# A hybrid GLA and RWKV-7 trunk: the first chunk spread over the opening, the block products put right behind the scores, the output tiles' last step moved back, the combined weights loaded from ScalarE's queue

## The reference, cut to what matters

```
h = rms_norm(x, norm_pre);  p = h @ w_in
# GLA group -> o_gla (4 heads, recurrence per token), gated by silu
prev = shift(p_shift);  xm = p_shift + mu * (prev - p_shift)          # token shift
r, kr, vr, wd, ad = split(xm)
w = exp(-0.606531 * sigmoid(w0 + tanh(wd) @ w_up));  a = sigmoid(a0 + ad @ a_up)
kk = normalised(kr * k_k);  kr = kr * (1 + (a - 1) * k_a)
S = S * (w - kk^T (a kk)) + v^T k;   y = S r                          # RWKV-7, 8 heads of 64
y = groupnorm(y) + sum(r * kr * r_k) * v;   o_rwkv = y * silu(z_r)
m = concat(o_gla, o_rwkv) @ w_out;   x = x + rms_norm(m, norm_post)
```

## Time and profile before

| | us |
|---|---|
| median of 3 runs | 2319.01 |
| lowest and highest | 2316.41, 2319.48 |
| the profiled execution | 2315.25 |
| its span | 2313.5 |
| TensorE busy | 2242.2 (97%) |
| VectorE busy | 1448.1 |
| ScalarE busy | 1284.4 |
| GpSimd busy | 578.2 |

### The profile page before, as it was taken

The page is one execution under the profiler, slowest core; times in us unless marked ns, Lnnn a source line. Parts: engine busy times, 40 slices in busy tenths (PEclk is TensorE's granted clock), DMA queues, the critical chain, the costliest instruction groups (busy, mean ns, idle before and its releaser), DMA issues. The chain is left out here.

```text
span 2313.5 us, 72365 instructions
## 1 busy us (share of the span) xinstructions
PE 2242.2 (97%) x31109; PEld 1704.8 (74%) x31109; DVE 1448.1 (63%) x2699; ACT 1284.4 (56%) x2757; POOL 578.2 (25%) x1070
## 2 busy tenths in 40 slices
PE   7999999999999998889999999999999998899998
PEld 5777777777777776777888888888888886544443
DVE  6444545444455554567777777777777777456675
ACT  8355555555555544645666666666666664343333
POOL 0000000000000000355555555555566565000000
PEclk9999999999999999999999999999999999999999
DMA  6212222222333331222222333232223234666675
GB/s 245 69 56 70 80 79 89 79 79 90 105 108 117 101 101 50 52 59 70 72 72 78 83 87 87 78 81 67 72 82 87 84 88 141 204 213 214 223 237 182
DMA packets 217278, 244.62 MB, mean 106 GB/s; under 512 B 110080, under 2 KB 159552, under 8 KB 212608
## 3 DMA queue, kind: packets, MB, share of 16 engines
q1 hardware_dynamic: 211056, 217.44, 30.8%
q10 hardware_dynamic: 5904, 22.55, 2.7%
HBM read 141.83 MB, written 98.10 MB: 104 GB/s over the span
## 5 line engine op out<-in xcount | busy, mean ns | idle before, releaser
L2111 PE MATMUL first<-h,w_hi 128*128 128x256 f16 (+1 forms) x2496 | 419.1, 272 | 0.0
L2070 POOL TENSOR_TENSOR r_inv_tmp<-r_inv 64x30 f32<-64x30 f32 (+14 forms) x480 | 265.8, 554 | 412.8 <-DMA r_inv<-scratch_blocks 376.5
L748 PE MATMUL d<-h,w_hi 128*128 128x256 f16 (+1 forms) x2176 | 351.6, 270 | 0.0
L2111 PE MATMUL first<-h,w_lo 128*128 128x256 f16 (+1 forms) x1248 | 337.8, 272 | 0.0
L748 PE MATMUL d<-h,w_lo 128*128 128x256 f16 (+1 forms) x1088 | 290.6, 270 | 0.0
L2072 POOL TENSOR_TENSOR r_inv<-r_inv,r_inv_tmp 64x30 f32<-64x30 f32 (+14 forms) x480 | 279.7, 583 | 37.6
L2111 PEld LDWEIGHTS first<-h,w_hi 128*128 128x128 f16 x2496 | 237.6, 98 | 50.4 <-issue 18.9
L748 PEld LDWEIGHTS d<-h,w_hi 128*128 128x128 f16 x2176 | 209.5, 98 | 33.6 <-issue 3.9
L2013 POOL MEMSET r_run_s<- 128x128 f16 x1 | 0.2, 204 | 917.9 <-POOLq L390 917.9
L748 PE MATMUL first<-h,w_hi 128*128 128x256 f16 (+1 forms) x1168 | 184.5, 268 | 5.0 <-DVE w_lo L1236 3.1
L2111 PE MATMUL r_d<-h,w_hi 128*128 128x256 f16 (+1 forms) x960 | 158.8, 271 | 0.8 <-DVE carry_s L2742 0.8
(11 more groups left out here) (393 smaller groups left out, 5129.2 us busy)
## 6 DMA issues: line engine op xcount, KB each, us to landing
h<-in_x SPq DMA_DIRECT2D x33, 512.0 KB, 3.7
r_ops<-in_x SPq DMA_DIRECT2D x33, 512.0 KB, 4.2
out_y<-r_ops SPq DMA_DIRECT2D x33, 512.0 KB, 7.4
scratch_hT<-h SPq DMA_DIRECT2D x16, 1024.0 KB, 7.0
h<-scratch_hT ACTq DMA_DIRECT2D x15, 1024.0 KB, 7.1
scratch_mg<-m_hl SPq DMA_DIRECT2D x33, 256.0 KB, 2.0
r_zr<-scratch_zr SPq DMA_DIRECT2D x33, 256.0 KB, 3.5
r_bon<-scratch_bonus SPq DMA_DIRECT2D x33, 256.0 KB, 5.1
```

What stands on the lines that cost most here:

```text
L748: mm = pe.matmul(out, lhs(k, a, w), rhs(k, a, w), start=(n == 0), stop=(n == len(terms) - 1))
L2070: step(pool.tensor_tensor(tmp, inv[0:n, 0:u, u:u + 1].to_broadcast([n, u, w]), inv[0:n, u:u + 1, u + 1:32].to_broadcast([n, u, w]), ALU.mult))
L2111: mm = pe.matmul(out, lhs(k, a, w), rhs(k, a, w), start=(m == 0), stop=(m == 3 * KT - 1))
```

## The change

It does five things. (1) The first chunk's ahead work on TensorE and VectorE no longer stands in one row at the end of the opening: `scores` follows the last piece of x6 of block 1, `inner` and `turn` the second piece of x10, `solve` and `join` the fourth; `masked`, `td` and `keep_w` likewise on VectorE. (2) In every body `xs` stands right behind `scores:4`, with four pieces of x8 ahead of both and two behind. On VectorE `clamp:1`, `k_prime`, `low:0`, `beta`, `a` and the two `strict` change places, on ScalarE `high:0`; on SyncE's queue `put_m:0` stands behind `inverse_back`. Since xs now ends before x8, `d_full` is numbered by the order in which rounds end (`FULL_NO`; every wait on `d_full` uses it, below only one is shown). (3) `o_done` of an output tile is held back until the next mark `done`, behind `keep_w`, or until the next `o_scaled`. (4) `get_tw` moves, with the same two loads, from SyncE's queue to ScalarE's, at points 3, 4, 6 and 8. (5) `mixed` of x12 in block 2 waits for a semaphore of its own engine.

```
     x0*4 meet:2 out scores:3 x0*2 kn inner:3 unknowns:2 turn:3 x2*4 out x2 advance:2 solve:3 join:3 x2 centre:1
-    x8*2 meet:3 scores:4 out x8*4 inner:4 unknowns:3 turn:4 xs variance:1 out x10*2 advance:3 solve:4 join:4
+    x8*4 meet:3 scores:4 xs out x8*2 inner:4 unknowns:3 turn:4 variance:1 out x10*2 advance:3 solve:4 join:4
     x10*4 out
 """.split()
 ACT_BODY = """
     -taken:x10 -load_h centred:0 taken:x12 odd:0 turned:1 tanh_w out z1:1 join_e:1 keep_y:0 taken:x4 tanh:lw0
     out tanh:la0 squares:0 tanh:lw2 tanh:la2 deviation:0 odd:1 out turned:2 k_factor taken:x6 z1:2 keep_y:1
-    join_e:2 affine:0 squares:2 out gamma taken:x0 odd:2 turned:3 high:0 rnorm:0 out rnorm:1 z1:3 join_e:3
+    join_e:2 affine:0 squares:2 out gamma taken:x0 odd:2 turned:3 rnorm:0 out rnorm:1 high:0 z1:3 join_e:3
     keep_y:2 taken:x2 centred:1 out taken:x8 odd:3 turned:4 out deviation:1 affine:1 z1:4 join_e:4 keep_y:3
     high:1 out
 """.split()
 DVE_BODY = """
-    zc:0 masked:1 -mixed:x10 -low:1 even:0 keep_w:1 mixed:x12 -bonus:0 out -r -bonus:1 next:0 join_o:1 lor_low mixed:x4
-    out masked:2 zc:1 decay out even:1 keep_w:2 normed:0 next:1 mixed:x6 join_o:2 gated:0 out masked:3 zc:2
-    clamp:0 even:2 mixed:x0 keep_w:3 clamp:1 low:0 out unit:0 unit:1 next:2 join_o:3 k_prime mixed:x2 out
-    -td masked:4 zc:3 beta a mixed:x8 strict:0 out strict:1 even:3 keep_w:4 normed:1 rkk next:3 join_o:4 gated:1
+    zc:0 masked:1 -mixed:x10 -low:1 even:0 keep_w:1 done mixed:x12 -bonus:0 out -r -bonus:1 next:0 join_o:1 lor_low mixed:x4
+    out masked:2 zc:1 decay out even:1 keep_w:2 done normed:0 next:1 mixed:x6 join_o:2 gated:0 out masked:3 zc:2
+    clamp:0 clamp:1 even:2 mixed:x0 keep_w:3 out done unit:0 unit:1 k_prime next:2 join_o:3 low:0 mixed:x2 beta out a
+    -td masked:4 zc:3 strict:0 out strict:1 mixed:x8 even:3 keep_w:4 done normed:1 rkk next:3 join_o:4 gated:1
     kappa out
 """.split()
 POOL_BODY = "-invert".split()
 SP_BODY = """
-    -put_m:1 out -bonus_out out out out get_gate:0 out put_m:0 -inverse_back out out blocks_out blocks_in
+    -put_m:1 out -bonus_out out out out get_gate:0 out -inverse_back out out put_m:0 blocks_out blocks_in
     get_gate:1 out
...
                 yield name, tile + (name == "get_gate")
+        elif name == "done":
+            yield "done", None
         elif name == "out":
...
 
+FIRST_CHUNK = {("x6", 6): ("scores",), ("x10", 2): ("inner", "turn"), ("x10", 4): ("solve", "join"),
+               ("mixed", "x6"): ("masked",), ("strict", "1"): ("td", "keep_w")}
+
+
 def opening_jobs(table):
 
     for b, back in ((0, False), (0, True), (1, False)):
+        pieces = {}
         for token in table if b else x6_first(table):
             if (token[0] == "-") == back:
                 token, _, n = token.lstrip("-").partition("*")
                 name, _, arg = token.partition(":")
-                if name not in STEP + AHEAD + POST + ("out", "td"):
-                    yield from script_jobs(name, arg, b, int(n or 1))
+                if name in STEP + AHEAD + POST + ("out", "done", "td"):
+                    continue
+                for job in script_jobs(name, arg, b, int(n or 1)):
+                    yield job
+                    pieces[name] = pieces.get(name, 0) + 1
+                    if b == 1:
+                        for first in FIRST_CHUNK.get((name, pieces[name] if name in XROUNDS else arg), ()):
+                            yield first, 0
 
 
 OUT_UNITS = [(tile, n) for tile in range(SINGLES) for n in range(12)]
-TW_LOADS = ((3, 0), (4, 1), (5, 2), (6, 3))
+TW_LOADS = ((3, 0), (4, 1), (6, 2), (8, 3))
 PRE_AT = (("get_pair", 12, 0), ("part_sum", 14, 3), ("part_high", 15, 3), ("part_low", 16, 3))
...
     done = [list(opening_jobs(table))]
+    held = []
     for b in range(NB + 1):
         jobs = []
         for job, arg in body_jobs(table, b):
+            if job == "done":
+                jobs += held
+                held = []
+                continue
             if job != "point":
                 if job != "room":
                     jobs.append((job, arg))
                 continue
             late = []
             while arg >= -1 and todo and todo[0][0] <= marks[arg]:
-                late.append(todo.pop(0)[2:])
+                unit = todo.pop(0)[2:]
+                if unit[0] == "o_done":
+                    held.append(unit)
+                    continue
+                if unit[0] == "o_scaled":
+                    late += held
+                    held = []
+                late.append(unit)
             if "fetch" in mine:
                 jobs += late
             for j, at in (("get_ow", OW_FROM), ("ow_high", OW_FROM + 1), ("ow_low", OW_FROM + 1)):
                 if j in mine:
-                    jobs += [(j, k) for k in range(2 * KT) if OW_AT[k] + at == arg]
+                    jobs.extend((j, k) for k in range(2 * KT) if OW_AT[k] + at == arg)
             if "get_tw" in mine:
...
 ROUND_KEYS = list(ROUND_NO)
+
+
+def full_order():
+
+    ends = {}
+    for n, (job, arg) in enumerate(j for jobs in PE_JOBS for j in jobs):
+        if job == "piece":
+            ends[arg[:2]] = n
+        elif job == "out":
+            ends["out", arg[0], arg[1] // 6] = n
+        elif job in ("xs", "kn", "bs"):
+            ends.update({(arg, job + str(k)): n for k in range(2)})
+        elif job == "rank":
+            ends.update({(arg[0], r % arg[1]): n for r in ("lw%d", "la%d")})
+        elif job == "centre":
+            ends.update({(job, arg, k): n for k in range(2)})
+        elif job == "variance":
+            ends[job, arg] = n
+    return sorted(ROUND_KEYS, key=ends.get)
+
+
+FULL_NO = {key: n for n, key in enumerate(full_order())}
 AT = {}
 for _e, _table, _mine in (("PE", PE_BODY, ()), ("ACT", ACT_BODY, ("part_high",)),
                           ("DVE", DVE_BODY, ("part_sum", "part_low"))):
     _first = [job for jobs in side_program(_table, _mine) for job in jobs if job[0] in _mine]
     AT.update({job: n + 1 for n, job in enumerate(_first + TAIL[_e])})
 EARLY = ("x12", "x4", "x6")
-assert [ROUND_NO[0, r] for r in EARLY] == [0, 1, 2]
+assert [ROUND_NO[0, r] for r in EARLY] == [FULL_NO[0, r] for r in EARLY] == [0, 1, 2]
 
...
                     get_npost()
-
-            def get_tw(i):
-                if i == 0:
-                    sp.wait_ge(d_full.sem, d_full.at(ROUND_NO[LAST, "x10"], 1))
-                    sp.wait_ge(ow_ok.sem, 2 * KT)
-                elif i == 2:
-                    sp.wait_ge(op_ok.sem, op_ok.at(LAST, 2))
-                    sp.wait_ge(kap_ok.sem, kap_ok.at(LAST, 2))
-                    sp.wait_ge(mix_ok.sem, mix_ok.at(LAST, 15))
-                elif i == 3:
-                    sp.wait_ge(bonus_out.sem, bonus_out.at(LAST, 3))
-                sp.dma_start(t_hi[i], c["tw_d"][i, 0]).then_inc(*ow_in[i].up(0))
-                sp.dma_start(t_lo[i], c["tw_d"][i, 1]).then_inc(*ow_in[i].up(0))
 
...
                 n = tiles(b) * P
-                out, m = bank_of((b, r)), ROUND_NO[b, r]
+                out, m = bank_of((b, r)), FULL_NO[b, r]
                 if h == 0 and third == 0:
...
                 run(jobs, does)
-                if n == 0:
-                    scores(0)
-                    inner(0)
-                    turn(0)
-                    solve_ahead(0)
-                    join_inverse(0)
             run(TAIL["PE"], does)
...
 
+            def get_tw(i):
+                if i == 0:
+                    act.wait_ge(d_full.sem, d_full.at(FULL_NO[LAST, "x10"], 1))
+                    act.wait_ge(ow_ok.sem, 2 * KT)
+                elif i == 2:
+                    act.wait_ge(op_ok.sem, op_ok.at(LAST, 2))
+                    act.wait_ge(kap_ok.sem, kap_ok.at(LAST, 2))
+                    act.wait_ge(mix_ok.sem, mix_ok.at(LAST, 15))
+                elif i == 3:
+                    act.wait_ge(bonus_out.sem, bonus_out.at(LAST, 3))
+                act.dma_start(t_hi[i], c["tw_d"][i, 0]).then_inc(*ow_in[i].up(0))
+                act.dma_start(t_lo[i], c["tw_d"][i, 1]).then_inc(*ow_in[i].up(0))
+
             def out_rstd(tile):
...
                     end = pair[:, :, n - 1:n]
+                if r == "x12" and b == 2:
+                    dve.wait_ge(kap_ok.sem, kap_ok.at(b - 1, 1))
                 dve.wait_ge(praw_ok.sem, praw_ok.at(b, 2 * k + 1 if k else 1))
...
                 if n == 0:
-                    keep_scores(0)
-                    turn_inverse(0)
-                    keep_w(0)
                     odd_join(0)
```

More of the change, by code:

```diff
@@ L1528, in side_program @@
         done.append(jobs)
-    done.append([j[2:] for j in todo])
+    done.append(held + [j[2:] for j in todo])
     return done
@@ L1911, in fetch @@
                 if tile >= 2:
-                    sp.wait_ge(d_full.sem, d_full.at(ROUND_NO["out", tile - 2, 1], 1))
+                    sp.wait_ge(d_full.sem, d_full.at(FULL_NO["out", tile - 2, 1], 1))
```

(6 more changed lines are left out.)

28 lines of the change are left out of this document (14 added, 14 removed).

## The result

The changed kernel takes 2343.78 us (median of 4 runs, 2340.74 to 2348.63), the kernel before 2318.42 (4 runs) beside it: ratio 1.0112, 95% interval 1.0094 to 1.0131. It is 25 us slower. I had forecast 2312.5 us, 6.5 us faster; the direction was wrong and the time lies outside my range.

The account below looks back on a forecast made before the run. TensorE, busy 97%, bounds the kernel; opening -3.4, xs -1.4, bank +9.1, body 0 +0.2, body 14 +1.7, end -12.7 give -6.5: profiled 2315.25 to 2308.8, plus 3.8 to the median, forecast 2312.5 us. Range 2301 to 2324.

Parts of the forecast that it names:

- x10's bank: Bodies 1 to 13: x10 waits for the carry's copy to release x8's bank, 0.7 us each, +9.1 us.
- `a` is done before the scores end: Bodies: VectorE finishes `a` 0.5 to 1.1 us before the scores end, so xs waits of 1.4 us go.
- +7.7 for the bodies: Thirteen like bodies: x10's bank wait +9.1 us together with xs waits -1.4 us.
- Body 14: Body 14: xs waits 2.4 us, x10 1.35, earlier waits of 1.4 and 0.69 go: +1.7 us net.
- The tile's store goes out some 3 us later; the slot is taken again far later: Output tiles at the end: the held-back step delays only the tile's store, while masked's waits shrink by 2.6 and 1.7 us.
- 7.7 us gained with its windows of low clock: Output tiles' last step at the end: waits -2.6 and -1.7 us plus two windows at clock 0.50 gone.
- Combined weights and the inverse's way back: End: inverse's store goes out 5.8 us earlier without weights' loads on SyncE's queue, -3.3 us, plus a clock window.
- Opening: Opening: waits of 1.85 and 1.22 us go, two xs waits grow, a clock window goes: -3.4 us together.
- The windows at 0.50: Half-clock windows go with their waits: one in the opening, -1.7 us, and three at the end, -5.1 us.
- The size of the base: Whole kernel: profiled execution 2315.25 us taken as base, with the median of runs 3.8 us above it.

Follow-up runs that it names:

- x_xs_inner2: As x_body_low, with the block products directly ahead of inner and VectorE's mixed of x8 ahead of strict and the output weights' low part: 2320.59 us, 1.0002.
- x_body_low: Kernel before plus change (2) with its SyncE move, but low:0 and high:0 back at their old places: 2342.56 us, 1.0109.
- x_odone: Kernel before plus only change (3), the output tiles' last step held back: 2327.93 us, 1.0027.
- The four kernels of the end: Kernel before plus change (4) and put_m's move, with and without the held-back step and the split residual load: 0.9996, 1.0014, 0.9991, 0.9972.
- x_end_split: Kernel before plus changes (3) and (4), put_m:0 behind inverse_back, and the residual's load issued 8 units later: 2316.87 us, 0.9991.
- x_tw: Kernel before plus change (4) and put_m:0 behind inverse_back, without the held-back step: 2320.03 us, 0.9996.
- x_tw_split: As x_tw, with the residual's load issued 8 units later as its own job: 2311.88 us, 0.9972.
- x_opening: Kernel before plus only change (1), the first chunk spread over the opening: 2324.04 against 2322.46 us, 1.0009.
- x_body_bank: As x_body_low, with TensorE's variance behind the two pieces of x10 instead of ahead: 2375.60 us, 1.0255.
- x_body_mix8: As x_body_bank, with VectorE's mixed of x8 ahead of the output weights' low part in body 14: 2372.08 us, 1.0244.

## Why the prediction was wrong, step by step

**x10's bank: right.** I had 0.7 us a body; the body near 1491 has 0.67 by the same count (its list of waits 0.4), and x_xs_inner2 takes the wait away by the distance that I named. The load of the first weights in the earlier trace rows was the sign of it.

**"`a` is done before the scores end": wrong.** I summed VectorE's durations and did not follow the moved `low:0` to the engine that waits for its reading to end. ScalarE's keep_y waits 1.8 us for it, and xs 0.46 us in most bodies. x_body_low takes 6.1 us away. In place of +7.7 for the bodies 16.3 came: 8.7 of the bank (thirteen times that body's 0.67), 5.7 of the wait for `a` as listed (less the 1.4 that the earlier trace rows had), and 3.3 that lie within the spread of single bodies.

**Body 14: the step of x10's wait was mis-sized**, 1.35 "by the same count" where it is 4.22. I had counted the low part of the output weights ahead of `a`, and overlooked that a second one now stands ahead of `mixed` of x8, behind a chain through ScalarE and TensorE's turn. The wait for `a` there, forecast at 2.4, measured 2.89. The two make 3.4 of the 4.6 us that body 14 is over its term; the rest I have not followed.

**"The tile's store goes out some 3 us later; the slot is taken again far later": wrong, and the dearest step.** I asked who needs the slot, and not what stands behind the store. SyncE's queue is in order: it waits for the held step before it issues the store, then for the store's landing before it issues the slot's next load, and the inverse's store and the pair's loads stand behind both. So the 4.3 us of masked's waits went, and waits of the same size took their place. x_odone, 6 us slower where I had 7.7 us gained with its windows of low clock, shows it alone. In my expectations I put the cost on the load. The four kernels of the end don't bear that out: the load's place costs 5.3 to 5.6 us with the held step or without it, so it is a delay that the kernel before has as well once the weights' loads are gone from the queue, and the held step costs 4.2 to 4.4 us with the load apart too. That this rest is the store's own place on the queue is argued from the rows of x_end_split; no run moves the store.

**Combined weights and the inverse's way back: the mechanism right**, where nothing else stands on the queue. (The sentence "as behind it on the queue were two loads" must read ahead of it.) I put -5.0; x_tw's profile has -3.7, its time -0.9 (-3.9 to +2.1), and x_tw_split -6.5 with the load apart. From the end of the store's issue to the load back 5.2 to 6.1 us pass with the weights' loads on ScalarE's queue and 5.3 to 5.9 with them on SyncE's, 5.5 in the earlier trace rows; the gain is the place on the queue. The rule of the Trainium skill that I weighed there (DMA: Bandwidth & Descriptors, "Issuing engines are not separate DMA queues") agrees with these rows. The remaining wait of 3.85 us at 2011 in the changed kernel was the tile's held store and the load behind it, not this.

**Opening: the waits went, but not the time.** -2.2 against the trace of before, which is lucky there; against the six other kernels with its opening the -3.4 came (100.2 us against 103.6 to 104.2). And still no gain in x_opening, as GpSimd's inversion of block 1, started by products that had not moved, comes last in body 0. I asked what hid behind the removed waits in the opening, and not in the body behind it. In the changed kernel body 0 lost 2.2 us: the states wait 2.02 us for VectorE behind `k_prime` (I had 1.1), and a window at clock 0.50 begins at the end of that wait; x_opening has no such wait and excludes part 1 as its cause.

**The windows at 0.50: the count was too firm.** I took three at the end and one in the opening as gone with their waits, and left out a fourth at the end, at 1935.5 behind a wait of 2.19. The one in the opening did go. The one at 944 is not the change's, although the wait ahead of it grew to 2.94: x_opening and the six other kernels with the old opening and bodies all have it, behind the same wait of 2.40 to 2.41 as in the earlier trace rows, and the trace of before is the one that lacks it. At the end a wait of 1.80 had one in the kernel before, and waits of 1.78 to 1.72 in x_tw and x_tw_split had none: near there it is chance, 1.7 us that no edit buys. The gain of 5.1 us that I booked for three windows rested on the waits ahead of them, and waits as long took their place.

**The size of the base.** The profile of before (2315.25) is one of the lucky executions, under all the runs shown: bodies with the same order took 61.5 to 66 us, and x_tw's trace loses 8 us more in them than the trace of before. What sets these extra microseconds, some of them issue waits at the head sums, I have not settled.

## What to carry to other kernels

Follow every moved instruction through three things: what it reads, and who overwrites that; what it releases, and what stands behind the release on an in-order queue; and which round of a rotating buffer is claimed next. A step moved back by some 3 us took its store with it, on a queue with urgent transfers behind, and that cost as much as the 4.3 us of waits that it freed. Where several transfers share a queue, put the one that may have to wait behind the urgent ones: this gave 5 us here, whatever else was changed. And test two edits in one stretch with and without each other before one is named as the other's cause.

## What the runs showed of the hardware

The length of TensorE's wait does not tell whether the granted clock falls to 0.50 (1.2 of 2.4 GHz) behind it, in any of these ranges:

- 1.7 to 1.8 us: a window of 3.4 us followed at 2034 in the kernel before, and none at 2030 in x_tw_split, behind 1.78 us with the same work around it.
- 2.4 us, the wait for `a` at 941 to 944: a window in seven kernels, none in the kernel before.
- 2.89 us, at 1935 in the changed kernel: none; the window came at 1944.6, within the next wait.
- 2.9 to 3.3 us, once in each of twelve bodies: one window in x_body_bank, two in x_body_mix8. At the end of the changed kernel waits of 3.85 to 5.29 us each had one, and so had the 3.09 and 3.67 of the earlier trace rows.

What else decides it these runs do not show.
